# Moving five of twelve modulation products from the matrix engine to VectorE, and all low parts of three projections with them

## The reference, cut to what matters

```python
h = rms_norm(x, g_ffn_pre)
gate, up = jnp.split(jnp.matmul(h, w_gate_up), [FFN_HIDDEN], axis=-1)   # FFN_HIDDEN = 2816
f = jnp.matmul(jax.nn.silu(gate) * up, w_down)
return x + rms_norm(f, g_ffn_post)
```

```python
mod_l = jnp.split((jax.nn.silu(c) @ w_ada[i] + b_ada[i])[:, None, :], 6, axis=-1)
mod_c = jnp.split((jax.nn.silu(c_ctx) @ w_ada[i] + b_ada[i])[None, None, :], 6, axis=-1)
hc = modulate(xc, mod_c[0], mod_c[1])
hl = modulate(xl, mod_l[0], mod_l[1])
```

## Time and profile before

| | |
|---|---|
| median of 3 runs | 1611.19 us (1610.83 to 1612.89) |
| the profiled execution's own time | 1614.68 us |
| its span | 1612.8 us |
| TensorE clock granted in it, mean | 0.995 |
| busy: PE, DVE, ACT, POOL | 97%, 49%, 38%, 30% |

### The profile page before, as it was taken

One profiled execution on the slowest core, in us unless ns is written; L12 is line 12 of the kernel. 1 busy time (PEld: TensorE's weight loads), 2 busy tenths in 40 slices (PEclk: granted clock), 3 DMA queues, 4 the chain that ended last, 5 costly groups with the idle time before them and its releaser, 6 DMA issues.

```text
span 1612.8 us, 24052 instructions
## 1 busy us (share of the span) xinstructions
PE 1566.7 (97%) x9726; PEld 1182.5 (73%) x9726; DVE 783.9 (49%) x1291; ACT 612.4 (38%) x1110; POOL 480.6 (30%) x318
## 2 busy tenths in 40 slices
PE   7999999999999999999999999999999999999987
PEld 6889899868889998888787888998644444444442
DVE  5654434246564332479767776446433333233223
ACT  4653444345553443455446665332211111111110
POOL 4432655434334544300126665353300000000000
PEclk9999999999999999999999999999999999999999
DMA  8644996537439986443427666957899999999994
GB/s 284 213 157 131 256 268 223 180 96 271 143 87 304 263 261 222 141 105 105 130 53 221 198 192 204 301 141 293 353 405 425 420 422 424 422 422 424 421 422 179
DMA packets 249972, 410.50 MB, mean 255 GB/s; under 512 B 7685, under 2 KB 196689, under 8 KB 228480
## 3 DMA queue, kind: packets, MB, share of 16 engines
q1 hardware_dynamic: 242864, 379.09, 67.7%
q10 hardware_dynamic: 3584, 19.86, 3.1%
q0 software_dynamic: 3408, 9.95, 1.7%
HBM read 407.72 MB, written 1.15 MB: 254 GB/s over the span
## 4 chain that ended last, share of the span: by engine, by line
PE 86%; DMA 6%; DVE 3%; issue 1%; POOL 1%; ACT 1%; SPq 0%; ACTq 0%; DVEq 0%; POOLq 0%
PE ps L144 84%; DMA arena<-in_w_expert_gate 2%; DMA arena<-in_w_expert_up 2%; PE ps L146 2%; DVE arena L154 1%; DVE arena L150 1%; DMA ring<-in_w_out 1%; POOL split_r L150 1%; DMA ring<-in_w_gate_up 1%; ACT split_r L148 1%; DVE split_r L150 1%; DMA rows<-in_b_s 0%; POOL arena_r L150 0%; ACT arena L148 0%; DVE arena_r L150 0%
## 5 line engine op out<-in xcount | busy, mean ns | idle before, releaser
L144 PE MATMUL ps<-arena_r,split_r 128*128 128x256 f32 (+1 forms) x2984 | 460.1, 288 | 2.6 <-POOL split_r L150 2.6
L150 POOL TENSOR_TENSOR split_r<-ring,split_r 128x1024 fp32r<-128x1024 f32 (+1 forms) x142 | 328.8, 2317 | 276.0 <-ACT split_r L148 247.0
L144 PEld LDWEIGHTS ps<-arena_r,split_r 128*128 128x128 f32 x2984 | 393.4, 188 | 23.2 <-issue 17.1
L148 ACT ACTIVATE split_r<-ring 128x1024 fp32r<-128x1024 f32 (+1 forms) x293 | 295.9, 1020 | 253.0 <-PE ps L144 183.6
L150 DVE TENSOR_TENSOR split_r<-ring,split_r 128x1024 fp32r<-128x1024 f32 (+1 forms) x151 | 225.8, 1497 | 290.6 <-ACT split_r L148 290.4
L144 PE MATMUL ps<-split_r,arena_r 128*128 128x512 f32 (+1 forms) x1520 | 340.8, 378 | 7.6 <-issue 3.1
L144 PEld LDWEIGHTS ps<-split_r,arena_r 128*128 128x128 f32 x1520 | 276.0, 189 | 54.4 <-issue 12.1
L144 PE MATMUL ps<-arena 128*64 128x512 f32 (+8 forms) x1232 | 303.3, 471 | 4.6 <-DVE arena L160 3.7
L144 PE MATMUL ps<-ring,arena 128*64 128x512 f32 (+2 forms) x688 | 226.1, 575 | 2.6 <-DMA rows<-in_w_expert_gate 0.9
L144 PE MATMUL ps<-hhh_r,split_r 128*128 128x256 f32 (+1 forms) x976 | 228.5, 322 | 0.0
L144 PEld LDWEIGHTS ps<-arena 128*64 128x64 f32 (+2 forms) x1232 | 120.9, 150 | 114.2 <-issue 101.2
(11 more groups left out here) (160 smaller groups left out, 1299.2 us busy)
## 6 DMA issues: line engine op xcount, KB each, us to landing
ring<-in_w_gate_up SPq DMA_DIRECT2D x88, 512.0 KB, 7.4
ring<-in_w_in SPq DMA_DIRECT2D x57, 512.0 KB, 5.4
arena<-in_w_ada SPq DMA_DIRECT2D x24, 1024.0 KB, 7.4
arena<-in_w_expert_gate SPq DMA_DIRECT2D x12, 2048.0 KB, 26.1
ring<-in_w_down SPq DMA_DIRECT2D x22, 1024.0 KB, 4.8
ring<-in_w_expert_up SPq DMA_DIRECT2D x11, 2048.0 KB, 25.1
ring<-in_w_expert_down SPq DMA_DIRECT2D x11, 2048.0 KB, 26.9
ring<-in_w_in SPq DMA_DIRECT2D x28, 768.0 KB, 5.9
```

Source lines behind the costliest of these rows:

```text
L144: made = e.matmul(*a, **k)
L148: made = e.activation(*a, **k)
L150: made = e.tensor_tensor(*a, **k)
```

## The change

1. DVE makes every low part from the gate and up projection to the end of the down projection, in both layers.
2. Units 4, 5, 9, 10 and 11 of the modulation are made by DVE: eight instructions for a unit, each of 128x512, that multiply a row block of `AW` by a column of `silu(c)` (one number for each partition) and add the running sum, which stands in a PSUM bank. Two are made in each of four steps. The bank is taken and held by PE for that time. The last instruction writes to `AD` in SBUF. PE's sum over the partitions stays, now with plain ones. Seven units stay with PE as before.
3. The steps at which the units are made change, as does what SP loads ahead of them: for a unit of DVE's it loads the weights up to unit m + 7.
4. Six units now lie in layer 0, and POOL's load of constants for layer 1 waits for unit 5 in place of 4.

```diff
-                if first["out", l][1] <= n < first["up", l, 0][1]:
+                if first["out", l][1] <= n < first["down", l][1] + 22:
                     return True
-                if first["z", l, 1][1] <= n < first["down", l][1] + 22:
+                if first["z", l, 1][1] <= n < first["out", l][1]:
                     return n % 2 == 0
...
-        ADA_AT = ({4: 0, 8: 1, 12: 2, 16: 3, 20: 4}, {3: 5, 6: 6, 9: 7, 12: 8, 15: 9, 18: 10, 20: 11})
+        ADA_AT = ({4: 0, 6: 1, 8: 2, 10: 3, 12: 4, 16: 5}, {3: 6, 5: 7, 7: 8, 9: 9, 13: 10, 17: 11})
+        ADA_BY_DVE = (4, 5, 9, 10, 11)
+        ada_begun = lambda l, m: [u for a, u in ADA_AT[l].items() if u not in ADA_BY_DVE and a == m]
+        ada_step = lambda l, m: [(u, m - a) for a, u in ADA_AT[l].items() if u in ADA_BY_DVE and a <= m < a + 4]
+        ada_ended = lambda l, m: [u for a, u in ADA_AT[l].items() if m == a + (1 if u not in ADA_BY_DVE else 4)]
...
-                        t.matmul(bk, C("selbc"), AD[u % 2], True, True).then_inc(*sig(s_mm, ("ada", u)))
+                        t.matmul(bk, ones, AD[u % 2], True, True).then_inc(*sig(s_mm, ("ada", u)))
...
-                        made = t.matmul(bk[:, 2 * c:2 * c + 2], AD[u % 2][:, tok(c)], C("selc"), True, True)
+                        made = t.matmul(bk[:, 2 * c:2 * c + 2], AD[u % 2][:, tok(c)], C("selc") if u not in ADA_BY_DVE else ones[:, 0:2], True, True)
...
                     bk = take(("up", l, m), ("ff", l, m))
+                    freed = [("am", u, "bank") for u, part in ada_step(l, m) if part == 0]
+                    for _, u, _ in freed:
+                        take(("am", u), ("am", u, "kept"), hold=True)
...
-                        made.then_inc(*sig(s_mm, ("split_done", n), *([("up", l, m)] if a else [])))
-                    if m - 1 in ADA_AT[l]:
-                        ada_sums(ADA_AT[l][m - 1])
-                    if m in ADA_AT[l]:
-                        ada_products(ADA_AT[l][m])
+                        made.then_inc(*sig(s_mm, ("split_done", n), *([("up", l, m)] if a else freed)))
+                    for u in ada_ended(l, m):
+                        ada_sums(u)
+                        if u in ADA_BY_DVE:
+                            drop(("am", u))
+                    for u in ada_begun(l, m):
+                        ada_products(u)
...
+            def modulation(u, part):
+                o, bk = AD[u % 2], B("am", u)
+                row = lambda k: AW[:, k // 4, k % 4, :]
+                if part == 0:
+                    v.wait_ge(*at("cs"))
+                    v.wait_ge(*at("am", u, "bank"))
+                for k in range(2 * part, 2 * part + 2):
+                    if k % 4 == 0:
+                        v.wait_ge(*at("ada_in", u, k // 4))
+                    if k:
+                        v.wait_ge(*v.latest)
+                    if k == 0:
+                        then(v.tensor_scalar(bk, row(k), cs[:, k, 0:1], None, ALU.mult))
+                    elif k < 7:
+                        then(v.stt(bk, row(k), cs[:, k, 0:1], bk, ALU.mult, ALU.add))
+                    else:
+                        v.wait_ge(*at("ada", u - 2))
+                        if u // 2 in (3, 4):
+                            made = v.stt(in_fours(o), by_four(row(k)), cs[:, k, 0:1], by_four(bk), ALU.mult, ALU.add)
+                        else:
+                            made = v.stt(o, row(k), cs[:, k, 0:1], bk, ALU.mult, ALU.add)
+                        then(made, ("am", u), ("am", u, "kept"))
...
                     gated(m)
-                    if m - 1 in ADA_AT[l]:
-                        modulated_by(ADA_AT[l][m - 1])
-                    if m in ADA_AT[l]:
-                        products_kept(ADA_AT[l][m])
+                    for u in ada_ended(l, m):
+                        modulated_by(u)
+                    for u in ada_begun(l, m):
+                        products_kept(u)
+                    for u, part in ada_step(l, m):
+                        modulation(u, part)
...
-                    g.wait_ge(*at("am", 4))
+                    g.wait_ge(*at("am", 5))
...
                         modulation(u, h)
-                    load_to(up[m + 5])
+                    load_to(up[m + (5 if u not in ADA_BY_DVE else 8)])
                     y.wait_ge(*at("am", u))
```

## The result

The changed kernel took 1603.91 us (median of 13 runs, 1601.84 to 1609.66), the kernel before 1612.47 us in 13 runs on the same chip (1610.83 to 1615.22). The ratio is 0.9955, with a 95% interval of 0.9947 to 0.9964: 7.3 us faster (5.8 to 8.5). The forecast was -8.85 us and 1602.3 us.

The account below looks back on a forecast made before the run. PE was taken as the bound, busy 1566.7 of 1612.8 us. Terms -9.25 + 0.1 + 0.3 = -8.85 us took the median from 1611.19 to 1602.3 us; own range 1600.8 to 1604.5, 8 in 10 within 1599.5 to 1606.5.

Parts of the forecast that it names:

- The forecast case: Whole kernel: PE loses five units' products, DVE's added work is free, small waits remain; -8.85 us, 1602.3 us, chance 0.65.
- Products: Gate and up loops of both layers: five units' products leave PE at 1.85 us each, -9.25 us.
- DVE's instructions: Steps with a DVE unit: multiply-and-adds at 0.75 us, 1.5 us a step, leave DVE's turn under PE's 5.88; 0 us.
- Low parts in loop and down stage: Gate and up loops and down stage: DVE makes all low parts at 1.23 us and PE does not wait; 0 us.
- The start of layer 0: Start of layer 0's gate and up loop: a wait for DVE's low part replaces POOL's 1.49 us wait; +0.1 us.
- The loads of `w_ada` in layer 1: Layer 1, after step 5: the load lands about 512.6, PE wants it at 512.7; +0.3 us, between 0 and 1.5.
- The rest: Later stages start from PE's progress, so they move as a whole; 0 us.
- A: Layer 0's start: unit 4's data land as before, latency sets it, POOL's 1.49 us wait goes; 1600.4 us, chance 0.12.
- B: `w_ada` loads get only 290 GB/s, units 7 and 8 about 2 us late each; 1606.0 us, chance 0.12.
- C: Running sum in PSUM makes DVE slower than PE; gain cancelled at 1.7 us an instruction, 1620.5 at 1.9; chance 0.05.
- 6.5 us of reserve: Steps with DVE units: a DVE up to 6.5 us late costs nothing, as PE has three quarters to do first.
- D: Moved places: small waits add up to 6 us or more, or products left no hole; about 1609 us, chance 0.06.

Follow-up runs that it names:

- e4: Changed kernel with the normed input's low part ahead of two of DVE's four low parts at each gate and up loop's start; 1601.41 us, ratio 0.9933.
- e1: Kernel before with only the low parts moved to DVE, modulation as it was; 1612.54 us against 1612.77, ratio 1.0.
- e7: Changed kernel with low parts as in the kernel before and the normed input's low part sooner on DVE; 1602.88 us, ratio 0.9937 to the kernel before.
- e2: Changed kernel with the low parts as in the kernel before, so only the five units' products move to DVE; 1601.08 us, ratio 0.9924.
- e8: The changed kernel again, unaltered, timed against the kernel before; 1604.27 us, ratio 0.9959.
- e3: Changed kernel with units 7 and 8 of layer 1 one step later (steps 6 and 8); 1602.27 us, ratio 0.9939 to the kernel before.
- e5: Changed kernel with six of the eight instructions of each DVE unit issued three times; 1621.6 us, ratio 1.0065 to the kernel before.
- e6: Changed kernel with a sixth unit (8) on DVE and the normed input's low part sooner; 1595.55 us, ratio 0.9893 to the kernel before.

## Why the prediction was right

The forecast case held: -8.85 us said, -7.3 (-8.5 to -5.8) by the ratio and -7.1 in the stage of the traces; 1603.91 us lies in the forecast's own range. The mechanism was right. The sum was 1.75 us too good by the traces. That it wasn't more was luck: one load cost 2.45 us more than said, and the products happened to give 0.55 us more. Step by step, from the timeline of PE (first product to start of the down projection, in each layer):

- **Products, -9.25 said.** e4 has no wait at all, so it shows the price. Layer 0 (one unit's products less, one sum more) went from 112.07 us before to 111.27, -0.80; layer 1 (four less, one sum less) from 622.14 - 498.54 = 123.60 to 611.74 - 497.14 = 114.60, -9.00. Together -9.80 for five units, 1.96 each and not 1.85. From its first instruction to the next matmul a unit still takes 1.86 us (515.44 to 517.30); what was missed is at its edges: the step between products and sum is 5.85 us, a plain one 5.75. The step of PE was 5.88 in the prediction, half of the 11.76 of the earlier trace rows, which is counted to the modelled end of the last matmul.
- **DVE's instructions, 0.75 us said, 0.756 measured.** The PSUM form was the right neighbour, and the 1.09 of the earlier trace rows was not. PE waited for none of DVE's results in any of these steps, and DVE had 1.3 us of waits in the turn shown. Price 0, as said.
- **Low parts in loop and down stage, 0 said.** e1 shows 0.0, and e7 against e4 0.9 at most, at the start of layer 0. The Trainium skill ("SBUF — State Buffer", "SBUF: two separate sides") describes the shared pair of ports as an exclusive lock. The traces agree: 1.225 us with POOL's low parts gone (median of 58 in layer 0, none over 1.227, so the "few near 2" didn't come either), 2.75 beside one of 2.42 in e2. But what that frees on DVE has no price as long as PE sets the pace.
- **The start of layer 0, +0.1 said, 0.0 measured** (19.47 us both times). The way there was right as well: one wait took the place of the other. In the stage the load went out 1.46 us later and not 1.65, as four low parts took 4.62 us and the two of before had already taken 3.15; PE had its normed input in time.
- **The loads of `w_ada` in layer 1, +0.3 said, 2.75 measured.** This is the term that was mis-sized, by 2.45 us, more than the 1.75 us by which the forecast was too good; the larger price of the products gave back 0.55. PE's time of want was right (512.7), the landing was not: 512.6 said, 515.3 (504.36 + 10.95). The forecast took the end of the fast stretch, 511, for the landing, and added 1.65 us. But in before the second half of that load was issued at 503.0 and landed 9.4 us later, at 512.4 (the loads of `w_ada` that start from 502.9 to 503.2 us):

```profile
DMA to landing us min/median/max: 9.4/9.4/9.4
```

  So 1.4 us of the miss stood in the trace of before already. Another 1.5 is that after's second half took 10.95 us to land, beyond the 9.5 of the earlier trace rows; it was issued 1.3 us later than before, at 504.36, a little less than the 1.65 said. "Level" was read as a small number, but where a transfer and its user are level, each microsecond of late issue or of a slower landing falls on PE in full: e8 gave 1.2, e2 0.4, after 2.75. The upper bound of 1.5 held nothing for the scatter of landing times. The Trainium skill's limit of some 358 GB/s ("DMA: Bandwidth & Descriptors", "Specifications") would have put 0.7 us more on the wait, for a slower `w_ada`. The first unit of layer 1 moved at 393 to 408 GB/s here too, above that limit. For unit 7 no run decides it: weights moved beside it, and its stretch shows 290 to 385 GB/s. What differs from before are dips, and when that second fast stretch begins (after, GB/s in slices of 1 us, 480 to 520 us):

```profile
GB/s 16 0 0 0 0 59 221 393 408 408 395 358 300 290 291 289 291 297 298 293 287 292 214 281 277 280 283 327 356 290 385 381 360 310 304 195 277 273 176 306
```

  In the earlier trace rows the second fast stretch runs from 504 to 511 us at 313 to 385 GB/s; here it runs from 507 to 513, with a slice of 290 in it, and slices of 214 and 195 stand on either side. e3 and e4 both take the wait away, one by asking later, one by issuing earlier.
- **The rest, 0 said.** From the sum of the parts, -0.80 (layer 0) and 117.42 - 123.60 = -6.18 (layer 1 with its wait), -7.0 of the stage's -7.1 are placed. The wait at line 160 differs among the kernels mainly by where the clock fell: 1.1 us in the five with a fall ahead of it, 1.8 to 2.2 in the five without. What lies behind the stage varied from 943 to 949 us among the executions, also between kernels that are the same there; it isn't counted for any.

**The rivals.** *A* (unit 4's latency, not the queue): ruled out by e4, where an issue 2.17 us earlier brought PE 2.02. *B* (`w_ada` late at several steps): its mechanism, a queue that gives no fast stretch, didn't come; it was late at one step only. Its time, 1606.0, was nearly as near as the forecast's (2.1 us off against 1.6). *C* (DVE the bound): no, with 1.3 to 1.5 us of waits in each turn of unit 4's. Its point of decision was wrong in the prediction, however. It claimed 6.5 us of reserve for each run of units; by e5 it is 1.4, for the low parts can be late, but the running sum is wanted by PE one step after its last part. In e5 DVE's turns were 3.2 + 3.5 + 3 x 4.9 = 21.4 us too long, and PE lost 18.7 of them, where the prediction's two reserves of 6 us would have left 9. *D*: no; the interval ends at -5.8 us.

## What to carry to other kernels

Work taken off an engine that runs without gaps returns its start-to-start time, here even with 0.1 us for each unit at its edges; the engine that takes it over pays nothing only up to the first consumer that wants the result, and that need not be the consumer whose slack was counted. A move of work that is free on its own engine can still delay a load, if a queue waits for something that is now behind it: one reordered line gave back 3.5 us by ratio here. And a load that is "level" with its user should be priced from its own landing and the scatter of such landings, not from the end of a fast stretch, or be asked for one step later. Last, what a fall of the clock costs is not what it adds to the piece in which it lies: the next wait may give half of it back, or all.

## What the runs showed of the hardware

- DVE multiplies by a column and adds at 0.756 us for 128x512 in float32 with a running sum read from and written to PSUM, 30 times within 3 ns. To SBUF at the end it is 0.748, and 1.168 for unit 9, whose last instruction reads and writes through the strided forms `by_four` and `in_fours`. e6 agrees: the median of its ends for units 8, 9 and 10 is 1.169, and the first two are strided.
- PE's granted clock fell to 0.50, the lower level of 1.2 GHz, within a stretch of some 4 us in eight of the ten profiled executions (twice in e5), at 1.56 to 1.75 us each in the piece of PE where it lay (the second of e5 apart). Each fall began within 1.5 us of the end of a pause of PE: of 2.59 us in after, e2, e3, e5 and e6, of 1.82 to 1.97 us at the next wait in e1, e4 and e7, of 1.86 us in layer 1's loop in e5. Before and e8 had the same pauses (2.59 and 1.79 us, 2.58 and 2.24 us) and no fall. What decides it wasn't found; a difference of up to 1.7 us between two single traces may be only this.
